# Forming the state transition, the solution parts and the readers of a chunked RWKV-7 scan ahead of its serial part

## The reference

```python
def step(s, inp):
    r_t, w_t, k_t, v_t, kk_t, a_t = inp
    s_kk = jnp.einsum('bhvk,bhk->bhv', s, kk_t)
    s = (s * w_t[:, :, None, :]
         - s_kk[..., None] * (kk_t * a_t)[:, :, None, :]
         + v_t[..., None] * k_t[:, :, None, :])
    return s, jnp.einsum('bhvk,bhk->bhv', s, r_t)
```

## Time and profile before

| | us |
|---|---|
| median of 3 runs | 1128.91 (1126.51 to 1131.95) |
| profiled execution | 1133.34 |
| its span | 1131.6 |
| PE busy in the span | 830.9 |
| DVE busy in the span | 491.6 |
| ACT busy in the span | 298.0 |

### The profile page before, as it was taken

One profiled execution on the slowest core, in us unless ns is written; L12 is line 12 of the kernel. 1 busy time (PEld: TensorE's weight loads), 2 busy tenths in 40 slices (PEclk: granted clock), 3 DMA queues, 4 the chain that ended last, 5 costly groups with the idle time before them and its releaser, 6 DMA issues. The chain is left out here.

```text
span 1131.6 us, 16557 instructions
## 1 busy us (share of the span) xinstructions
PE 830.9 (73%) x6694; PEld 514.7 (45%) x6694; DVE 491.6 (43%) x1062; ACT 298.0 (26%) x662; POOL 142.9 (13%) x148
## 2 busy tenths in 40 slices
PE   3599999999326546675765657599937999999910
PEld 3354556555215435554553546345524544544400
DVE  1300076753558357746864682534361111212136
ACT  1401122312442453273346225101101111111124
POOL 3000000000150040022004000000002222222031
PEclk9599999999557567666666785899956999999965
DMA  8922430640600000000000004150017999999562
GB/s 292 346 100 75 148 117 34 224 150 1 206 1 2 3 1 23 3 2 4 1 4 1 4 2 189 48 197 38 19 38 284 376 360 352 359 358 360 186 224 93
DMA packets 42148, 147.86 MB, mean 131 GB/s; under 512 B 5999, under 2 KB 8566, under 8 KB 37366
## 3 DMA queue, kind: packets, MB, share of 16 engines
q1 hardware_dynamic: 32854, 75.45, 18.7%
q0 software_dynamic: 9216, 71.31, 17.0%
HBM read 131.77 MB, written 20.74 MB: 135 GB/s over the span
## 5 line engine op out<-in xcount | busy, mean ns | idle before, releaser
L2188 PE MATMUL banks<-arena 128*128 128x512 f32 x304 | 157.4, 600 | 0.0
L1736 PE MATMUL banks<-arena 128*128 128x512 f32 x288 | 129.6, 604 | 1.1 <-ACT arena L1358 1.1
L2187 PEld LDWEIGHTS banks<-arena 128*128 128x128 f32 x304 | 57.8, 192 | 73.4 <-issue 71.5
L1736 PEld LDWEIGHTS banks<-arena 128*128 128x128 f32 x288 | 55.6, 194 | 71.4 <-issue 69.8
L1760 PE MATMUL banks<-arena 128*128 128x512 f32 x144 | 65.1, 595 | 1.1 <-DVEq L1176 1.0
L1604 DVE TENSOR_TENSOR arena<-arena,banks 128x256 f32<-128x256 f32 x18 | 7.6, 420 | 123.4 <-ACT arena L1364 116.8
L2187 PE MATMUL banks<-arena 128*128 128x128 f32 x304 | 59.8, 279 | 1.5 <-ACT arena L201 1.5
L2067 DVE TENSOR_TENSOR arena<-arena 128x641 f32<-128x641 f32 x15 | 12.4, 827 | 99.6 <-ACT arena L1934 99.6
L2057 DVE SCALAR_TENSOR_TENSOR arena<-arena 128x640 f32<-128x640 f32 x60 | 49.7, 877 | 0.0
L1049 PE MATMUL banks<-arena,ident 128*64 128x64 f32 x256 | 18.3, 277 | 42.1 <-DVE arena L831 29.4
L2188 PEld LDWEIGHTS banks<-arena 128*128 128x128 f32 x304 | 46.6, 194 | 0.0
(11 more groups left out here) (333 smaller groups left out, 1634.6 us busy)
## 6 DMA issues: line engine op xcount, KB each, us to landing
arena<-in_ada_w_dram SPq DMA_DIRECT2D x12, 2048.0 KB, 12.5
arena<-in_w_in_dram SPq DMA_DIRECT2D x5, 2048.0 KB, 14.5
slot_rows<-arena SPq DMA_DIRECT2D x18, 512.0 KB, 8.1
arena<-modulations SPq DMA_DIRECT2D x8, 512.0 KB, 7.4
h_rows<-arena SPq DMA_DIRECT2D x5, 512.0 KB, 2.6
out_dram<-arena SPq DMA_DIRECT2D x5, 512.0 KB, 2.6
arena<-in_x_sample_dram SPq DMA_DIRECT2D x4, 512.0 KB, 10.8
arena<-in_w_out_dram SPq DMA_DIRECT2D x1, 2048.0 KB, 8.1
```

The source lines that it names most:

```text
L1736: x = T_.matmul(ps[2 + s][:, :], hT[:, s, c, :], wgu[:, s, c, :], start=(c == 0), stop=(c == KD - 1))
L2187: T_.matmul(ctx_[:, 0:P], w, h1T[:, k, 0:P], start=(k == 0), stop=(k == KD - 1))
L2188: x = T_.matmul(lat[:, :], w, h1T[:, k, P:T], start=(k == 0), stop=(k == KD - 1))
```

## The change

For each pair of slots, three new staging steps are put behind `gram` and `keys`. `xloc` multiplies the masked products by the values. `wqx` multiplies the inverse by both the scaled queries and that product, which gives the part of the solution that doesn't depend on the state, and a matrix QT. `mr` forms the 64x64 transition (identity plus QT times keys) and the readers (queries plus QT times masked products). With these the chain of a slot is one accumulated group of products, keys by solution and transition by state, and one multiplication by the decay that writes both directions of both heads. The outputs `y` are formed for 128 tokens at once, from the kept states. The temporary buffers go from two to three, the chain has one bank per step instead of two.

The schedule is cut in another way: `gram` and `keys` of a pair no longer stand in its own preparation but behind it. `early` holds the first five rounds of staging of pair m with the first steps of preparation of m+1 (and the head norm of m-1); `late` holds the rest of the staging, the chain and the outputs of m with the second steps of m+1, the 30 substitution steps among them.

```diff
-        gmask = sb("causal_mask", [P, 2 * 2 * 64])
-        earlier = sb("earlier_token", [P, P])
+        gmask = sb("causal_mask", [P, 2, 2, 2, 64])
+        repeat = sb("repeated_identity", [P, P])
...
-        EXEC = [2, 0, 3, 1, 4, 5, 6, 7, 8, 9]
+        CHAIN = [2, 0, 3, 1, 4, 5, 6, 7, 8]
+        STAGES = [1, 0, 2, 3, 4]
+        TILES_Y = [0, 2, 3, 1, 4]
...
+            for k in range(len(STAGES) + 3):
+                tick = []
+                for name, lag in (("mr", 3), ("wqx", 2), ("xloc", 1), ("gram", 0), ("keys", 0)):
+                    if 0 <= k - lag < len(STAGES):
+                        tick.append((name, m, STAGES[k - lag]))
+                ticks.append(tick)
...
+            early = [x for t in ticks[0:5] for x in t]
+            late = [("init", m)] + ticks[5] + [("chain", m, 2), ("chain", m, 0)] + ticks[6] + [("chain", m, 3), ("chain", m, 1), ("state_out", m)] + \
+                ticks[7] + [("chain", m, 4), ("y", m, 0), ("chain", m, 5), ("chain", m, 6), ("y", m, 2), ("chain", m, 7), ("y", m, 3),
+                            ("chain", m, 8), ("y", m, 1), ("y", m, 4)]
...
+            if m < 3:
+                SCHEDULE += spread(early, extra + first_steps(m + 1)) + spread(late, second_steps(m + 1))
+            else:
+                SCHEDULE += spread(early, extra) + late
...
-            return pp[TEMP_AT[key] % 2]
+            return pp[TEMP_AT[key] % 3]
...
                 elif k == "keys":
-                    act.wait_ge(*at("u_zero", (m, q)))
+                    j = STAGES.index(q)
+                    if j >= 2:
+                        act.wait_ge(*at("wqx_mm", (m, STAGES[j - 2])))
...
+                    a.copy(qx[:, j % 2, :, :, 0:64], t[:, 768:1024].rearrange("p (i h n) -> p i h n", i=2, h=2)).then_inc(*up("read_keys", st))
+                elif k == "xloc":
+                    act.wait_ge(*at("xloc_mm", (m, q)))
+                    a.copy(qx[:, j % 2, :, :, 64:128], temp(st)[:, 0:256].rearrange("p (i h n) -> p i h n", i=2, h=2)).then_inc(*up("read_xloc", st))
+                elif k == "wqx":
+                    act.wait_ge(*at("wqx_mm", (m, q)))
+                    a.copy(qt[:, :, :, :], t[:, :, :, 0:64]).then_inc(*up("read_wqx"))
+                    for d in range(2):
+                        a.copy(uv[URows[d], 2 * q:2 * q + 2, d, :].rearrange("p i (h n) -> p i h n", h=2), t[URows[d], :, :, 64:128]) \
+                            .then_inc(*up("read_wqx", st))
+                elif k == "mr":
+                    act.wait_ge(*at("mr_mm", (m, q)))
+                    a.copy(mt[:, 2 * q:2 * q + 2, :, :].rearrange("p i d c -> p d i c"),
+                           t[:, :].rearrange("p (d n) -> p d n", d=2)[:, :, 0:128].rearrange("p d (i c) -> p d i c", i=2)).then_inc(*up("read_mr"))
+                    for d in range(2):
+                        a.copy(qr[m % 2][:, d, 1, r_cols(d, q)], t[:, d * 512 + 128:d * 512 + 256]).then_inc(*up("read_mr", st))
...
-                            v.tensor_scalar(dst, src, f[0:64, :], None, ALU.mult).then_inc(*up("state_next", (m, s)))
...
+                    v.tensor_tensor(states[:, next_slot(s), :, :], chain_bank(m, s)[:, 0:P].rearrange("p (d c) -> p d c", d=2), end_scale(m, s), ALU.mult) \
+                        .then_inc(*up("state_next", (m, s)))
...
+                elif k == "mr":
+                    pe.wait_ge(*at("read_wqx", ("wqx", m, q)))
+                    for d in range(2):
+                        T_.matmul(t[:, d * 512:d * 512 + P], ident[:, :], repeat[:, :], start=True, stop=False, skip_group_check=True)
+                        T_.matmul(t[:, d * 512 + P:d * 512 + 2 * P], ident[:, :], qr[m % 2][:, d, 1, r_cols(d, q)], start=False, stop=False,
+                                  skip_group_check=True)
...
+                elif k == "chain":
+                    for d in range(2):
+                        for h in range(2):
+                            x = T_.matmul(bank[hs, d * HD:(d + 1) * HD], ktok[:, s, d, hs], uv[:, s, d, hs], start=(d == 0),
+                                          stop=(s == 0 and d == 1), skip_group_check=True)
+                    if s:
+                        pe.wait_ge(*(at("read_init", ("init", m)) if s == 2 else at("state_next", (m, s - 1))))
+                                x = T_.matmul(bank[hs, d * HD:(d + 1) * HD], mt[hs, s, d, :], states[hs, s, d, :], start=False, stop=(d == 1),
+                                              skip_group_check=True)
```

More of the change, by code:

```diff
@@ L336, in prep_steps @@
             out += [(("sub", m, j), 0.45 + 2 * (31 - j) * j / 960) for j in range(1, 31)]
-            return out + [(("turn", m), 2.5), (("off", m), 0.3), (("merge_a", m), 0.3), (("merge_b", m), 0.3)]
-        def stage_steps(m, q):
-            return [("gram", m, q), ("keys", m, q)]
-        SLOT_FREE = {0: 3, 1: 2, 2: 5, 3: 7, 4: 9}
-        def chain_steps(m):
-            out, late = [], []
-            for i, s in enumerate(EXEC):
-                out.append(("x", m, s))
-                out += late
-                out += [("u", m, s), ("s", m, s)]
-                late = [("y", m, s)]
-                if s == 1:
-                    late.append(("state_out", m))
-                if i == 8 and m < 3:
-                    late.append(("init", m + 1))
-            return out + late
+            return out + [(("turn", m), 4.0), (("off", m), 0.3), (("merge_a", m), 0.3), (("merge_b", m), 0.3)]
@@ L397, in build @@
             k = st[0]
-            if k in ("low_rank", "key_norm", "gram", "keys", "diag", "off", "merge_a", "merge_b", "bonus", "init", "state_out"):
-                TEMPS.append(st)
-            elif k == "head_bonus":
+            if k in ("low_rank", "key_norm", "gram", "keys", "xloc", "wqx", "mr", "y", "diag", "off", "merge_a", "merge_b", "bonus", "init",
+                     "state_out", "head_bonus"):
                 TEMPS.append(st)
@@ L558, in scan_pool @@
             g.memset(wb[:, :, :, :, :], 0.0).then_inc(*up("wb_zero"))
-            g.memset(nothing, 0.0).then_inc(*up("state_zero"))
-            g.memset(state[:, :, :, :, :], 0.0).then_inc(*up("state_zero"))
+            g.memset(ec[:, :, :], 1.0).then_inc(*up("end_one"))
             for st in SCHEDULE:
                 k = st[0]
-                if k == "keys":
-                    _, m, q = st
-                    if m:
-                        for s in (2 * q, 2 * q + 1):
-                            pool.wait_ge(*at("y_mm", (m - 1, s)))
-                    g.memset(uv[:, 2 * q:2 * q + 2, :, :], 0.0).then_inc(*up("u_zero", (m, q)))
-                elif k == "decay":
+                if k == "decay":
                     _, m, d = st
@@ L810, in scan_dve @@
                     if m:
[L811 to L818 removed]
+                        dve.wait_ge(*at("y_mm", (m - 1, TILES_Y[-1])))
@@ L870, in scan_pe @@
                 k = st[0]
-                if k in ("low_rank", "key_norm", "gram", "keys", "diag", "off", "merge_a", "merge_b", "bonus", "init", "state_out",
-                         "head_bonus"):
+                if st in TEMP_AT:
                     temp_free(pe, st)
@@ L1107, in build @@
         ones = take(P)
+        earlier = take(P)
         w1, w2_ = [take(NT) for _ in range(2)]
@@ L1251, in post_pool @@
             g.memset(ones, 1.0).then_inc(*up("pool_did", "ones"))
+            g.memset(earlier, 1.0).then_inc(*up("pool_did", "earlier"))
+            pool.wait_ge(*at("pool_did", "earlier"))
+            g.affine_select(out=earlier, in_=earlier, pattern=[[1, P]], compare_op=ALU.is_gt, fill=0.0, base=0, channel_multiplier=-1) \
+                .then_inc(*up("pool_did"))
             g.iota(slot_no, pattern=[[1, P]], base=0, channel_multiplier=0, allow_small_or_imprecise_dtypes=True) \
```

411 lines of the change are left out of this document (180 added, 231 removed).

## The result

| | before | after |
|---|---|---|
| median | 1129.45 us (1126.51 to 1131.95, 4 runs) | 1113.00 us (1111.36 to 1114.85, 4 runs) |
| ratio, 95% interval | | 0.9856 (0.9824 to 0.9887) |
| profiled execution, span | 1133.34, 1131.6 | 1114.46, 1112.6 |

A forecast was written before the change was run, and what follows sets the result against it. In the scan's long stretches no engine was full; the path through waits, mainly the preparation, was taken as the bound. Terms -9.4, -1.9 and +11.7 gave +0.4 us: 1133.7 profiled, 1129 as median, range 1101 to 1152.

The forecast's parts named there:

- Start and pair 0: Up to pair 0's merges: staging maskings and a wait go (10.3 us), a third PSUM memset adds 0.9; net -9.4.
- E is 35.8: Five staging rounds in `early`, from merges to table load: carried by PE, beginning at the slower clock, 35.8 us per pair.
- The lower bound for the three new groups: Least price of `xloc`, `wqx` and `mr` together in `early`: 2.4 us, against 3.9 taken and 6.5 at most.
- From the table load to the diagonal, 23.4: Table load to diagonal transpose: pair 0's 24.7 us less two key-norm waits, plus three DVE operations of 0.3 each; 23.4.
- To `turn`, 28.5: Diagonal transpose to `turn`: 34.7 us less 10.3 of staging, plus seven chain steps and one 2 us wait; 28.5.
- To the end of the merges, 12.3: From `turn` to the end of the merges: 11.9 us plus 0.4 for two last `y` tiles.
- Pair 3: Last merges to pair 3's head statistics: staging now precedes the chain, 48.4 us against 36.7, so +11.7.
- Behind the scan: After pair 3's head statistics: nothing changes, 0 us; early loads, wanting about 13.5 us, still land before the scan's end.
- The periods: Three stretches between successive pairs' merges: 100.0 us each, 300.0 together against 301.9 before, so -1.9.
- rival 2: Scan periods: overlap better than added up, sum -28 us, 1101; half of that, -14, is 1115; chance 0.30.
- no wait behind the diagonal: A reason given for the faster case: no wait after the diagonal transpose, helping bring table load to merges' end to 61 us.
- Rival 1: In `early`: PE slower and waiting for ACT, stretch 42 us, 1151; or row tiles take turns, 1148; chance 0.28.

The follow-up runs named there:

- xloc_twice: Changed kernel with every product of `xloc` issued twice: 1123.63 us, ratio 0.9947 to the kernel before.
- act_twice: Changed kernel with the ACT copy of `xloc` done once more into a free part of its PSUM buffer: 1114.84 us, ratio 0.9864.
- bonus_behind: Changed kernel with pair 1's low-rank steps and squares in pair 0's substitution, plus bonus products of pairs 1 to 3 moved to the start of `early`: 1112.69 us.
- scale_twice: Changed kernel with each of the 36 chain scalings on DVE done once more into a free part of its bank: 1117.42 us, ratio 0.9898.
- two_temps: Changed kernel with two temporary PSUM buffers instead of three: 1141.58 us, ratio 1.0087 to the kernel before.
- before_staging_behind: Kernel before, own algorithm, with `gram` and `keys` taken out of the preparation and put behind the merges: 1139.23 us, ratio 1.0077.
- filled_wait: Changed kernel with unneeded PE products put into waits, eight ahead of one `mr` and three ahead of the diagonal products: 1118.8 us, ratio 0.9903.

## Why the prediction was wrong

The mechanism was the predicted one, and most terms held; two sizes were off, both on the same side.

- *Start and pair 0*, -9.4: measured -10.1 (384.5 to 374.4). Right.
- *E is 35.8.* This step failed: 32.2 to 32.7, together 9.9 us less over three pairs. In period 2 (32.7 us) it comes apart like this:
  - The slower level was to last 9 us and cost 3. Only `keys` behind the merges ran at it, 3.0 us for 1.6 (-1.6).
  - The second key norm, 1.1, runs beside the last copies of ACT (-1.1).
  - The other groups, each from its start to the next one's, take 3.4 for `mr` (priced 4.2), 5.1 for `wqx` and `xloc` (6.1), 7.9 for `keys` (8.8), 4.7 for the low-rank steps (5.2) and 4.4 for the four later `gram` (4.6). Of these 3.4 us the 1.4 of overlap is no gain, since the prediction took it off by itself; about 2 are left (-2.0), spread over all of them; one `mr` was priced 2.1 and takes 1.6 to 1.8.
  - Against that stand 0.6 for five transposes of the head steps on PE, which the prediction had on DVE alone, and 0.55 for a second wait for ACT, and 0.4 of smaller terms (+1.6).

  Together -3.1, as measured. `xloc_twice` and `act_twice` show that the rest of the step was right: PE carries E, ACT doesn't. The lower bound for the three new groups was also added up wrong: 0.43, 0.43 and three times 0.43 are 2.15 and not 2.4. What the three take (0.68, 1.09 and 1.6, so 3.4, priced 3.9) lies within the bounds either way.
- *From the table load to the diagonal, 23.4.* Failed as well: 21.0 to 22.1, -6.0 over three. The term was taken from pair 0. The three short DVE operations priced at 0.9 cost nothing: the start state stands in a wait of DVE, the first chain scaling beside other work (419.19, with the product behind it 0.2 shorter), the second in the wait for the diagonal products. And that wait in pair 0 held a stop of PE of 0.97, which pairs 1 and 3 don't have and pair 2 has at 0.81: from the last product of DVE to the transpose are 4.3 us there, and 2.9, 4.0 and 2.9 here. 0.9 and 1.4, 0.3 and 1.4 give the 21.0, 22.1 and 21.0 measured to 0.1.
- *To `turn`, 28.5*, with a first chain step 2 us late and no other wait: 28.7, 28.8, 28.4, the wait 2.84. Right, and `bonus_behind` shows the cause. `scale_twice` shows that a step costs no round trip. The 2.26 for the bonus products was the slower level of pair 0, taken without a word on the clock; at the faster one they take 1.25 (434.63). That PE was at the slower level here too is luck of the forecast.
- *To the end of the merges, 12.3*: 12.3, 12.3, 11.1.
- *Pair 3*, +11.7: measured +10.4. *Behind the scan*, 0: -0.6; the early loads landed in the last stretch (DMA share 0.33).

The periods sum to 283.2 for 300.0, and that is nearly the whole miss: -19.0 us of span where +0.4 was forecast. It is the half case of rival 2, named at 1115; of its reasons the faster level in E and the low-rank products side by side were seen, "no wait behind the diagonal" was not. Rival 1 asked for PE at the slower level or for row tiles that take turns; neither was there. An E near 42 does occur, but with two buffers (39.9 without the table load, as rival 1 counts) or a stop at the start of E (39.4).

One thing missing in the prediction decided more than either term: it let E be bound by PE without a price for the buffer that makes this true. By `two_temps` it is worth some 28 us, more than the whole gain.

Before and after compared: the reorder (`before_staging_behind`) is +0.8%, the third buffer in the old kernel +1.4%, the change without the third buffer +0.9%. So none of these three steps gains, and all together do: the short chain step frees a bank pair, the third buffer lets PE run E at 93 to 97%, and only so does the staging in front cost less than it gives back behind. The new chain in the old order was not run, so that the new order is needed too is argued and not shown.

## What to carry to other kernels

When work is moved into a stretch where one engine does everything, count that engine's groups at the price of the faster clock, take the time at the slower one from a trace (here 5 us behind the merges, and 15 where the stretch began with a stop), and then ask which buffer would make it stop: one buffer fewer cost 28 us, where the whole change gained 16. A product in an in-order list costs what stands behind it, so move work to a place where nobody waits (pair 0's substitution: -5.7 us), not merely to an engine that is idle on average. Before filler work that raises the clock is called worth nothing, look whether the products that somebody waits for got faster; here they had not.

## What was not expected of the hardware

- Two row tiles that write different partitions of one PSUM bank ran side by side: 16 products in 0.68 us with one bank and with two.
- The ten bonus products of 2 columns take 2.26 us at a granted clock of 0.50 and 1.25 at 1.00 (434.63), though by their columns they would be among the shortest groups. Beside them in pair 0 of the kernel before stand ten weight loads of 128x128 that are busy for 2.21 of the 2.26 us.
- With 2.27 us of waiting and 2.27 us of narrow products put in front of E, PE was at the slower level until 15 us behind the merges instead of 5, and E grew by 7.0, not by 4.5.
- In `filled_wait` PE was at 1.00, stood for 2.57 us, and was at 0.50 for the products behind that.
- PE stops in the middle of the diagonal group in some pairs, for 0.81 to 2.04 us, and the profile shows nothing that it waits for. The cause is open.
